# Splitting the last modulation of a mixer and expert block, and moving its gate half into the router steps

## The chip, the cores and the metric

The kernel runs on one core of a Trainium2 chip. The metric is the device time of one execution in microseconds (us); 1724.52 us is the median of three runs of the kernel before (1724.0 to 1725.7). The engines are TensorE (PE, with its weight loads as PEld), VectorE (DVE), ScalarE (ACT), GpSimd (POOL) and SyncE (SP), whose queue issues the large weight transfers. The core's 16 DMA engines share the transfers.

## The reference

A sequence of 256 tokens of width 1024 in fp32 passes two blocks. The first is conditioned on a vector `c`:

```
mod = (silu(c) @ w_ada + b_ada)            # 6 x 1024
shift1, scale1, gate1, shift2, scale2, gate2 = mod
h = rms_norm(x, norm1_g) * (1 + scale1) + shift1
proj = h @ w_in                            # conv, stick-breaking and forgetting attention
x = x + gate1 * (rms(y) * out_norm_g @ w_out)
h2 = rms_norm(x, norm2_g) * (1 + scale2) + shift2
logits = h2 @ router_w + router_b          # 32 experts, top 4, softmax of the four
out_e = swiglu(h2 @ w1_e + b1_e) @ w2_e + b2_e
x = x + gate2 * sum over experts of gate_e * out_e
```

The second block is a Fourier and convolution mixer, a gated feed-forward part, a pooling mixer, a second feed-forward part and a norm. `w_ada` is 1024 x 6144. An expert's weights are 1024 x 2048 and 1024 x 1024 values, 12.6 MB, and all 32 experts are read.

## The kernel before, in words

All large weights go through a ring of 14 places of 1 MB in on-chip memory. `ring_order` lists the units in the order in which SP issues them, and each unit takes the place of the one 14 before it. SP waits until that one has been used (`emptied`) and issues the new one; it does so strictly in order. The order of the first block is: `w_ada` third 0 (8 units), `w_in` (16), `w_ada` third 1 (8), `w_out` (4), `w_ada` third 2 (8), and then the experts. Of each expert there are eight units of the first matrix (`w1`) and four of the second (`w2`); the first two `w1` units of the next expert stand ahead of the `w2` units of this one. So `w1` units 0 and 1 of expert 0 take the places of `w_ada` units, and `w1` unit 2 of expert 1 takes the place of `w1` unit 0 of expert 0.

A third of `w_ada` is 2048 columns. An `ada_unit` multiplies 128 rows of it by 128 values of silu(c); its four matmuls of 512 columns go to four strips of 32 partitions of one bank (L478). Third 2 holds scale2 and gate2, third 1 holds gate1 and shift2. `mod_done` adds the bias (L1331).

Everything on an engine runs in program order, and semaphores tie the engines together. The stages that the change touches are:

- **Output projection.** Eight pieces (`out_piece`, L458 to L460, twelve matmuls each) accumulate in banks 0 to 3. ACT rounds a piece of `w_out` (L2114) and DVE takes the rest (L1315) into two buffers, so a piece can be prepared when the one two before it has been used. The eight `ada_unit` calls of third 2 stand between the pieces. Then the columns of shift2 and scale2 are turned into per-partition form (L734), piece 7 follows, gate2 is spread to 128 partitions (L740), and shift2 is multiplied with the router's weights (L746).
- **Residual.** DVE multiplies the four quarters by gate1 (L1686) and adds them to x (L1689). Ahead of that its program has the rest of the expert biases (L1665), two small constant matrices `J` and `S_` (L1667, L1669) and the slot numbers (L1670 to L1677).
- **Router.** PE transposes x (L757), multiplies by the router's weights (L764) and sums the parts (L769, "logits"). DVE finds the four best experts of each token (L1710 to L1729, "chosen"). PE counts each token's place in its expert (L772 to L774, "places"), and DVE makes the selection matrix of the first four experts (L1736, "ST"). PE gathers the tokens of experts 0 to 3 with 32 matmuls (L916, L921).
- **Expert 0.** PE starts with two `w1` units (L811), then counts the tokens of each expert (L932, L933), turns the places (L936), makes the slot row (L799) and the slot gates (L789) and turns the gates (L944). After that PE waits for DVE's copies of the turned gates (`gT`, L1847), reads the count of expert 0 into a register (`value_load`) and takes a branch: an expert with more than 64 tokens gets a second part. The branch ends with `skip` (L466), which adds to a semaphore from PE's instruction stream. A `w1` place is only free after the unit has been used and this second part has been run or skipped: for units 0 and 1 at the branch ahead of unit 2, for units 2 and 3 at the branch after unit 3, for units 4 to 7 at the branch after unit 7.

```
            if kind == "w1":
                return [name, ("w1b", name[1], (0, 0, 1, 1, 2, 2, 2, 2)[name[2]])]
```

## Time and profile before

| | us |
|---|---|
| median of 3 runs | 1724.52 |
| lowest, highest | 1724.0, 1725.7 |
| the profiled execution's own time | 1724.98 |
| its span | 1723.2 |
| PE busy | 1577.0 (92%) |
| DVE busy | 676.6 (39%) |
| ACT busy | 430.1 (25%) |

The span is the time from the first to the last instruction of the profiled execution; its own time is the one to which a time for the changed kernel can be compared, and it lies 0.46 us above the median. The page divides the span into 40 slices of 43 us. The experts run from about slice 5 to slice 27. The mean granted clock of TensorE is 0.973 of full speed. The queue of SP moves 530 of the 533 MB. A share of DMA of 1.0 (or slightly above, as it is modelled) means that all 16 engines move data all the time.

### The profile page before, as it was taken

Reading aid. Unit: us, or ns where it says so; the run is one execution under the profiler, and the core shown is the slowest. Engines: PE = TensorE matmul, PEld = TensorE weight load, DVE = VectorE, ACT = ScalarE, POOL = GpSimd, SP = SyncE. Lnnn points to the kernel's source line nnn. Section 1 sums busy time; section 2 is a strip of 40 time slices with the busy share of each in tenths; the row PEclk is TensorE's granted clock in tenths of the full one; section 3 lists DMA queues with packets and bytes.
Section 4 is the critical chain, followed back from the end, with each engine's and each line's share of the span. In section 5 each row is a group of like instructions: output and inputs, shape, how many; then the busy total and the mean of one; then the engine's idle time right before and its main releaser. Section 6 shows DMA issues by size and latency. Waiting matters only on the chain.

```text
span 1723.2 us, 21783 instructions
## 1 busy us (share of the span) xinstructions
PE 1577.0 (92%) x8617; PEld 884.4 (51%) x8617; DVE 676.6 (39%) x947; ACT 430.1 (25%) x670; POOL 43.1 (2%) x68
## 2 busy tenths in 40 slices
PE   6999899999999898999989888886998999889998
PEld 3887533333333223333223222224848998689986
DVE  3475522232312222232212212124766565356653
ACT  3564311101110000110101000003425444244443
POOL 3032000000000000000000000000000000000000
PEclk9999899999999999999999999997998999989999
DMA  9648979999999999999999999996335555355540
GB/s 362 184 162 303 372 283 418 415 417 416 415 417 415 417 416 416 417 415 417 415 415 415 410 418 412 415 407 215 121 122 171 181 186 192 101 167 179 192 147 25
DMA packets 151411, 533.46 MB, mean 310 GB/s; under 512 B 9693, under 2 KB 72820, under 8 KB 115280
## 3 DMA queue, kind: packets, MB, share of 16 engines
q1 hardware_dynamic: 149664, 530.18, 78.9%
q8 instruction: 123, 2.02, 0.5%
q0 software_dynamic: 1584, 0.94, 0.3%
q14 instruction: 40, 0.33, 0.1%
HBM read 530.02 MB, written 1.05 MB: 308 GB/s over the span
## 4 chain that ended last, share of the span: by engine, by line
PE 39%; DMA 14%; DVE 2%; ACT 1%; issue 1%; SPq 0%; DVEq 0%; ACTq 0%
DMA ring<-in_w_mlp 14%; PE ps L460 8%; PE ps L458 8%; PE ps L459 8%; PE ps L811 7%; PE ps L829 1%; PE ps L1199 1%; PE ps L836 1%; PE ps L1141 1%; PE ps L782 1%; PE ps L1280 1%; PE ps L1113 0%; PE ps L1294 0%; PE ps L1149 0%; DVE arena L2039 0%
## 5 line engine op out<-in xcount | busy, mean ns | idle before, releaser
L811 PE MATMUL ps<-ring,arena 128*64 128x512 f32 x2048 | 495.9, 606 | 25.6 <-DMA ring<-in_w_mlp 22.2
L811 PEld LDWEIGHTS ps<-ring,arena 128*64 128x64 f32 x2048 | 128.2, 136 | 273.0 <-issue 197.0
L829 PE MATMUL ps<-ring,arena 128*64 128x512 f32 x1024 | 239.0, 602 | 31.3 <-DMA ring<-in_w_mlp 26.6
L1315 DVE TENSOR_TENSOR wl<-ring,wh 128x1024 fp32r<-128x1024 f32 x132 | 161.3, 1225 | 138.4 <-ACT wh L2114 138.4
L458 PE MATMUL ps<-hth,wh 128*128 128x256 f32 x704 | 199.4, 283 | 1.3 <-DVE htl L1965 1.3
L460 PE MATMUL ps<-hth,wl 128*128 128x256 f32 x704 | 200.2, 284 | 0.0
L459 PE MATMUL ps<-htl,wh 128*128 128x256 f32 x704 | 198.6, 282 | 0.0
L1787 DVE TENSOR_TENSOR arena<-ps,arena 128x1024 f32<-128x1024 f32 x70 | 85.6, 1225 | 259.8 <-PE ps L836 246.1
L2114 ACT ACTIVATE wh<-ring 128x1024 fp32r<-128x1024 f32 x132 | 139.0, 1059 | 150.1 <-PE ps L460 150.1
L829 PEld LDWEIGHTS ps<-ring,arena 128*64 128x64 f32 x1024 | 69.4, 137 | 195.4 <-issue 122.4
L1807 DVE TENSOR_TENSOR arena<-ps,arena 128x512 f32<-128x512 f32 x34 | 23.5, 692 | 360.2 <-PE ps L829 357.0
L458 PEld LDWEIGHTS ps<-hth,wh 128*128 128x128 f32 x704 | 134.4, 191 | 2.0 <-DVE htl L1965 2.0
L459 PEld LDWEIGHTS ps<-htl,wh 128*128 128x128 f32 x704 | 134.9, 192 | 0.0
L460 PEld LDWEIGHTS ps<-hth,wl 128*128 128x128 f32 x704 | 134.1, 190 | 0.0
L2364 ACT ACTIVATE arena<-arena 128x512 f32<-128x512 f32 (+1 forms) x34 | 21.0, 617 | 318.1 <-DVE arena L1793 318.1
L2400 ACT ACTIVATE obh<-arena 128x512 fp32r<-128x512 f32 x30 | 18.9, 630 | 317.0 <-DVE arena L1807 317.0
L458 PE MATMUL ps<-wh,fth 128*128 128x512 f32 x176 | 69.8, 396 | 0.0
L459 PE MATMUL ps<-wl,fth 128*128 128x512 f32 x176 | 69.6, 396 | 0.0
L460 PE MATMUL ps<-wh,ftl 128*128 128x512 f32 x176 | 69.5, 395 | 0.0
L2348 ACT ACTIVATE arena<-ps,arena 128x256 f32<-128x256 f32 x60 | 30.5, 559 | 138.5 <-PE ps L782 131.5
L458 PE MATMUL ps<-wp,ht 128*128 128x384 f32 (+1 forms) x128 | 46.3, 362 | 3.8 <-DVE ht L1379 2.3
L460 PE MATMUL ps<-wp,ht 128*128 128x384 f32 (+1 forms) x128 | 44.6, 348 | 0.0
(409 smaller groups left out, 1761.2 us busy)
## 6 DMA issues: line engine op xcount, KB each, us to landing
ring<-in_w_mlp SPq DMA_DIRECT2D x384, 1024.0 KB, 21.4
ring<-in_w_ada SPq DMA_DIRECT2D x24, 1024.0 KB, 14.2
ring<-in_ffn_w_gate SPq DMA_DIRECT2D x22, 1024.0 KB, 5.2
ring<-in_ffn_w_up SPq DMA_DIRECT2D x22, 1024.0 KB, 5.2
ring<-in_ffn_w_down SPq DMA_DIRECT2D x22, 1024.0 KB, 4.8
ring<-in_w_in SPq DMA_DIRECT2D x10, 768.0 KB, 12.4
ring<-in_w_in_ab SPq DMA_DIRECT2D x6, 1024.0 KB, 12.3
ring<-in_w_out SPq DMA_DIRECT2D x4, 1024.0 KB, 8.0
```

Source lines behind the costliest of these rows:

```text
L458: pe.matmul(o, lh, rh, start=first, stop=False)
L459: pe.matmul(o, lh, rl, start=False, stop=False)
L460: return pe.matmul(o, ll, rh, start=False, stop=last)
L811: t = pe.matmul(PS[64 * g:64 * g + 64, HB[hb][ns], :], x[:, k8, :], u[:, f:f + 512], start=False, stop=k8 == 7)
L829: t = pe.matmul(PS[64 * g:64 * g + 64, 3, :], a4[:, kc, 64 * kg:64 * kg + 64], u[:, c, g * 512:(g + 1) * 512], start=k8 == 0, stop=k8 == 7)
L1315: dve.tensor_tensor(l, src, h.bitcast(F32), ALU.subtract).then_inc(*V.tick((st, "lo", n)))
L1787: dve.tensor_tensor(x, PS[:, b:b + 2, :], x, ALU.add).then_inc(*tick(name))
L1807: dve.tensor_tensor(OBF, PS[:, bank, :], G2R, ALU.mult).then_inc(*tick(n_f))
L2114: act.activation(h, src, ACT.Copy).then_inc(*S.tick((st, "hi", n)))
L2348: act.activation(XGT[b % 2][:, k, :], PS[:, bank, (k % 2) * 256:(k % 2) * 256 + 256], ACT.Identity, scale=a2[:, k:k + 1], bias=sh2[:, k:k ...
L2364: act.activation(SIG[:, 0:n], GLU[:, 0:n], ACT.Sigmoid, scale=1.702).then_inc(*Q.tick(name))
L2400: act.activation(OBH[0], OBF, ACT.Copy).then_inc(*S.same())
```

## The change

Third 2 of `w_ada` is read as two halves, `scale2` and `gate2`, of four units each. A unit is again 1 MB, but 256 rows by 1024 columns. The new function `ada_half` multiplies such a unit with four matmuls of 512 columns: strips 0 and 2 take the even 128 rows, strips 1 and 3 the odd ones, and `S_` (here a matrix that adds the two strips of a half) joins them when the result is turned or spread. The same number of bytes is read.

- The four `scale2` units stand ahead of pieces 3, 4, 5 and 6. The turn of scale2 and shift2 moves behind piece 7, in between the transposes of x.
- The four `gate2` units move into the router: two behind the logits, one behind the token counts, one behind the gather. Their sum goes to bank 3, and its bias is loaded again by GpSimd into part 0 of `modr`, once that has been used and zeroed (`ab2`).
- DVE makes `J` and `S_` at the very start and the slot numbers in the projection stage; the rest of the biases goes between two pieces of `w_out`.
- The token counts and the turn of the places move ahead of the gather. The rest of h (`h_rest`) for tokens 0 to 127 moves ahead of "pos".
- Spreading gate2 and turning the gates move behind the branch that frees the places of `w1` units 0 and 1, and PE's wait for `gT` moves into the loop over the experts; so do DVE's copies of the gates and the product with `b2`.
- GpSimd issues six bias transfers instead of four at the start, and two more with a memset of 128 x 512 values later.

```diff
-    order += ... [("out", kk) for kk in range(4)] + [("ada", 2, k) for k in range(8)]
+    order += ... [("out", kk) for kk in range(4)] + [(w, k) for w in ("scale2", "gate2") for k in range(4)]

+            def ada_half(name, k, bank):
+                u = rows_of((name, k), 2)
+                pe.wait_ge(*landed((name, k)))
+                for q in range(2):
+                    for c in range(2):
+                        p = 64 * q + 32 * c
+                        t = pe.matmul(PS[p:p + 32, bank, :], cTp[:, 2 * k + c, :], u[:, c, q * 512:(q + 1) * 512],
+                                      start=k == 0, stop=k == 3)
+                t.then_inc(*P.tick((name, k)))
...
+            pe.wait_ge(*done("cB"))
             for i in range(2):
                 t = pe.matmul(PS[:, 1, i * 32:(i + 1) * 32], parts[:, i * 128:(i + 1) * 128], J, start=True, stop=True)
             t.then_inc(*P.tick("logits"))
+            ada_half("gate2", 0, 3)
+            ada_half("gate2", 1, 3)
             pe.wait_ge(*done("chosen"))
...
+            pe.matmul(PS[0:1, 1, 0:32], CT(C_ONE, 1), gt[:, 0, :], start=True, stop=False)
+            pe.matmul(PS[0:1, 1, 0:32], CT(C_ONE, 1), gt[:, 1, :], start=False, stop=True).then_inc(*P.tick("counted"))
+            ada_half("gate2", 2, 3)
+            pe.wait_ge(*done("pos"))
...
+            ada_half("gate2", 3, 3)
             pe.wait_ge(*done("SB1 0"))
             pe.wait_ge(*done("B1S"))
+            pe.wait_ge(*done("cnt"))
             mlp1_bias(0, 0)
...
-            for i in range(2):
-                t = pe.transpose(PS[0:32, 2, 256 + i * 128:384 + i * 128], gate[:, i, :], ident)
-            t.then_inc(*P.tick("gate turned"))
-            pe.wait_ge(*done("gT"))
...
             second_gather(0, here > CAP)
             second_start(0, here > CAP)
+            pe.wait_ge(*done(("xgt", 0, 2)))
+            for g in range(2):
+                t = pe.matmul(PS[64 * g:64 * g + 64, 6, :], S_[:, g, 0:1].bitcast(F32).to_broadcast([128, 64]),
+                              modr[:, 0, :], start=True, stop=True)
+            t.then_inc(*P.tick("gate2"))
+            for i in range(2):
+                t = pe.transpose(PS[0:32, 2, 256 + i * 128:384 + i * 128], gate[:, i, :], ident)
+            t.then_inc(*P.tick("gate turned"))
...
+            pool.wait_ge(*done("mod turned"))
+            pool.memset(modr[:, 0, :], 0.0).then_inc(*G.tick("mod 0 zeroed"))
+            pool.wait_ge(*done("mod 0 zeroed"))
+            for q in range(2):
+                small("ab2", modr[64 * q:64 * q + 1, 0, :], I["b_ada"][:, 5120 + 512 * q:5632 + 512 * q])
...
-            for k in range(8):
-                ada(2, k)
+            for w, c in (("scale2", 4096), ("gate2", 5120)):
+                for k in range(4):
+                    fill_rows((w, k), I["w_ada"][0], k * 256, 2, c, 1024)
```

PE's program before, from the last matmul of output piece 6 to the first two of piece 7; L734 turns shift2 and scale2:

```order
L460 MATMUL ps<-wo_63,yl 128x512
L734 MATMUL ps<-arena 128x2 x8
L458 MATMUL ps<-wo_65,yh 128x512
L459 MATMUL ps<-wo_66,yh 128x512
L460 MATMUL ps<-wo_65,yl 128x512
```

And from the last matmul of piece 7 to the logits (L769), with the spreading of gate2 (L740), the shift's logits (L746, L747), the transposes of x (L757), the constant row (L760) and the router's product (L764):

```order
L460 MATMUL ps<-wo_65,yl 128x512
L740 MATMUL ps<-arena 64x512 x2
L746 MATMUL ps<-arena 32x1 x8
L747 MATMUL ps<-arena 32x1
L757 MATMUL ps<-arena 128x128 x16
L760 MATMUL ps<-arena 128x32
L764 MATMUL ps<-arena 32x256 x8
L769 MATMUL ps<-arena 128x32 x2
```

PE's program now, from the last matmul of piece 7 to the logits (now L784); L745 turns scale2, L752 is half of the transposes of x, L760 now turns shift2, L776 is the router's product:

```order
L460 MATMUL ps<-wo_65,yl 128x512
L745 MATMUL ps<-s,arena 128x2 x4
L752 MATMUL ps<-arena 128x128 x8
L760 MATMUL ps<-arena 128x2 x4
L752 MATMUL ps<-arena 128x128 x8
L770 MATMUL ps<-arena 32x1 x8
L771 MATMUL ps<-arena 32x1
L776 MATMUL ps<-arena 32x256 x8
L779 MATMUL ps<-arena 128x32
L784 MATMUL ps<-arena 128x32 x2
```

The turn of both rows stood ahead of piece 7; now it is in two parts behind it, and the spreading of gate2 is gone from this place.

PE's program before, from the logits to the branch of expert 0 (L957 reads the count); L772 to L774 are the places, L916 and L921 the gather, L811 the first two `w1` units, L932 and L933 the counts, L936 turns the places, L799 and L789 make slot row and slot gates, L944 turns the gates:

```order
L769 MATMUL ps<-arena 128x32 x2
L772 MATMUL ps<-arena 128x32
L773 MATMUL ps<-arena 128x32
L774 MATMUL ps<-arena 128x32
L916 MATMUL ps<-st,hh 128x256 x16
L921 MATMUL ps<-st,hl 128x256 x16
L804 MATMUL ps<-b1s,sb_83 128x512 x2
L811 MATMUL ps<-ring,arena 64x512 x8
L932 MATMUL ps<-arena 1x32
L933 MATMUL ps<-arena 1x32
L936 MATMUL ps<-arena 32x128 x2
L799 MATMUL ps<-post,s 128x256
```

The same stretch now, up to the gather; L718 is `ada_half`, L789 to L791 the places, L793 and L794 the counts, L798 turns the places:

```order
L784 MATMUL ps<-arena 128x32 x2
L718 MATMUL ps<-ring,arena 32x512 x8
L789 MATMUL ps<-arena 128x32
L790 MATMUL ps<-arena 128x32
L791 MATMUL ps<-arena 128x32
L793 MATMUL ps<-arena 1x32
L794 MATMUL ps<-arena 1x32
L718 MATMUL ps<-ring,arena 32x512 x4
L798 MATMUL ps<-arena 32x128 x2
L941 MATMUL ps<-st,hh 128x256 x16
```

And from the gather to the read of the count (L975); L829 is the bias, L836 the first two `w1` units, L824 and L814 slot row and slot gates:

```order
L946 MATMUL ps<-st,hl 128x256 x16
L718 MATMUL ps<-ring,arena 32x512 x4
L829 MATMUL ps<-b1s,sb_83 128x512 x2
L836 MATMUL ps<-ring,arena 64x512 x8
L824 MATMUL ps<-post,s 128x256
L814 MATMUL ps<-arena,st 64x1 x16
L975 TENSOR_LOAD arena
```

Three gate units and the counting steps now stand ahead of the gather, the fourth gate unit behind it, and nothing is left between the slot gates and the read of the count.

## Rows read from the trace of the kernel before

**Rows 1.** The page, part 2, what the DMA engines moved.

```profile
GB/s 362 184 162 303 372 283 418 415 417 416 415 417 415 417 416 416 417 415 417 415 415 415 410 418 412 415 407 215 121 122 171 181 186 192 101 167 179 192 147 25
```

**Rows 2.** Busy time by stretch: each engine's, granted clock, DMA share, GB/s.

```profile
196.00:210.00 14.00, 9.38 (x47) 6.65 (x46) 9.37 (x31) 8.14 (x16) 0.00 (x0) 0.50 1.01 409
210.00:212.00 2.00, 2.00 (x12) 2.00 (x12) 1.61 (x5) 0.00 (x0) 0.00 (x0) 0.56 0.40 158
212.00:224.00 12.00, 8.52 (x79) 4.89 (x79) 5.33 (x14) 1.97 (x4) 0.00 (x0) 0.92 0.01 1
224.00:226.00 2.00, 2.00 (x6) 0.67 (x7) 0.69 (x1) 0.00 (x0) 0.00 (x0) 0.50 0.52 119
...
234.00:240.00 6.00, 6.00 (x29) 1.78 (x29) 2.55 (x3) 1.28 (x1) 0.00 (x0) 1.00 0.61 220
240.00:260.00 20.00, 19.47 (x94) 6.94 (x92) 4.50 (x7) 3.07 (x6) 0.00 (x0) 1.00 1.01 397
```

**Rows 3.** PE in order of time, last expert: start, duration, idle before.

```profile
1160.93 1.94 PE L811 MATMUL ps<-ring,arena 128*64 128x512 f32 x8 [0.52 <-DMA ring<-in_w_mlp]
```

**Rows 4.** Waits of SP's queue, 195 to 260 us: total, times, longest.

```profile
SPq L2624 <- PEq L466: 44.3, 4, 29.5
```

**Rows 5.** PE in order of time, from the logits to expert 0.

```profile
202.64 1.03 PE L769 MATMUL ps<-arena 128*128 128x32 f32 x4 [0.71 <-DVE arena L1701]
206.00 0.64 PE L772 MATMUL ps<-arena 128*128 128x32 f32 x2 [2.33 <-DVE arena L1729]
...
208.53 3.59 PE L916 MATMUL ps<-st,hh 128*128 128x256 f32 x16 [1.04 <-DVE st L1736]
211.96 2.07 PE L921 MATMUL ps<-st,hl 128*128 128x256 f32 x16
...
214.42 3.65 PE L811 MATMUL ps<-ring,arena 128*64 128x512 f32 x16
...
219.42 1.12 PE L789 MATMUL ps<-arena,st 128*64 128x1 f32 x32
...
223.85 6.10 PE L811 MATMUL ps<-ring,arena 128*64 128x512 f32 x16 [2.98 <-PEq L466]
```

**Rows 6.** PE in order of time, the output projection.

```profile
156.55 1.06 PE L478 MATMUL ps<-ring,arena 128*32 128x512 f32 x8
...
182.11 1.92 PE L478 MATMUL ps<-ring,arena 128*32 128x512 f32 x16
...
186.86 1.84 PE L734 MATMUL ps<-arena 128*128 128x2 f32 x16
188.56 0.49 PE L458 MATMUL ps<-wo,yh 128*128 128x512 f32 x1
```

**Rows 7.** DVE in order of time, from the bias rest to the residual.

```profile
189.02 2.47 DVE L1665 TENSOR_TENSOR b1s<-arena,b1s 32x1024 fp32r<-32x1024 f32 x2
...
192.85 0.69 DVE L1686 TENSOR_TENSOR arena<-ps,arena 128x512 f32<-128x512 f32 x1
...
197.64 0.69 DVE L1689 TENSOR_TENSOR arena<-arena 128x512 f32<-128x512 f32 x1
```

**Rows 8.** PE in order of time, the first `w_ada` unit of the program.

```profile
7.00 1.93 PE L478 MATMUL ps<-ring,arena 128*32 128x512 f32 x8 [2.92 <-DMA ring<-in_w_ada]
```

**Rows 9.** DVE in order of time, the copies of the turned gates.

```profile
221.12 0.85 DVE L1847 COPY arena<-ps 32x256 f32<-32x256 f32 x2
```

**Rows 10.** DVE and POOL in order of time, where work moves to.

```profile
14.04 0.15 DVE L1344 TENSOR_SCALAR arena<-arena 128x1 f32<-128x1 f32 x1 [8.16 <-ACT arena L2128]
...
85.49 0.56 DVE L1387 COPY arena<-ps 128x384 f32<-128x384 f32 x1 [2.34 <-PE ps L460]
...
41.39 1.39 POOL L2561 MEMSET arena<- 128x1536 f32 x1 [26.35 <-DVE ht L1379]
```

**Rows 11.** POOL and PE, the gains issued last and first used.

```profile
10.59 0.96 POOL L2538 DMA_DIRECT2D arena<-in_fox_k_g  x2
...
26.23 0.26 PE L500 MATMUL ps<-arena 4*128 4x4 f32 x1
```

More of the change, by code:

```diff
@@ L114, in ring_order @@
     first = len(order)
-    order += [("ada", 1, k) for k in range(8)] + [("out", kk) for kk in range(4)] + [("ada", 2, k) for k in range(8)]
+    order += [("ada", 1, k) for k in range(8)] + [("out", kk) for kk in range(4)] + [(w, k) for w in ("scale2", "gate2") for k in range(4)]
     order += [("w1", 0, 0), ("w1", 0, 1)]
@@ new lines, in _, with x_turn @@
+            t.then_inc(*P.tick("scale2 turned"))
+            def x_turn(i, ns):
+                pe.wait_ge(*done(("x1", i, ns)))
+                for k in range(4 * ns, 4 * ns + 4):
+                    b, o = 4 + k // 2, (k % 2) * 256 + i * 128
+                    t = pe.transpose(PS[:, b, o:o + 128], X[:, i, k * 128:(k + 1) * 128], ident)
+                    if i == 1 and k % 2:
+                        t.then_inc(*P.tick(("x turned", k // 2)))
+            pe.wait_ge(*done(("yL", 3)))
+            x_turn(0, 0)
@@ L738, in _ @@
+            x_turn(1, 0)
+            for cc in range(4):
+                t = pe.matmul(PS[:, 6, 2 * cc:2 * cc + 2], modr[:, 1, cc * 128:(cc + 1) * 128], ident[:, 64:128:32],
+                              start=True, stop=True)
+            t.then_inc(*P.tick("shift2 turned"))
+            pe.wait_ge(*done("a2"))
             pe.wait_ge(*done("s2"))
-            for g in range(2):
-                t = pe.matmul(PS[64 * g:64 * g + 64, 5, :], sel_w(2 + g)[:, 0:64], modr[:, 2, :], start=True, stop=True)
@@ L748, in _ @@
+            pe.matmul(PS[0:32, 1, 100:101], rbrow, CT(C_ONE, 1, 0, 1), start=False, stop=True).then_inc(
                 *P.tick("shift logits"))
-            P = sig["pe_route"]
-            for ns in range(2):
-                pe.wait_ge(*done("Jc" if ns else "G2R"))
-                for i in range(2):
-                    pe.wait_ge(*done(("x1", i, ns)))
-                    for k in range(4 * ns, 4 * ns + 4):
-                        b, o = 4 + k // 2, (k % 2) * 256 + i * 128
-                        t = pe.transpose(PS[:, b, o:o + 128], X[:, i, k * 128:(k + 1) * 128], ident)
-                        if i == 1 and k % 2:
-                            t.then_inc(*P.tick(("x turned", k // 2)))
@@ L760, in _ @@
-            pe.matmul(PS[:, 1, 64:96], CT(C_ONE, 128, 0, 32), Jc, start=True, stop=True).then_inc(*P.tick("shifts"))
             for k in range(8):
@@ L2358, in _ @@
             xgt(0, 2, 6)
+            act.wait_ge(*done("gate2"))
+            act.activation(G2R, PS[:, 6, :], ACT.Copy).then_inc(*S.tick("G2R"))
             S, S2 = sig["act_moe"], sig["act_moe2"]
```

173 lines of the change are left out of this document (92 added, 81 removed).

## The prediction

> **What bounds the kernel now.** I read the page's row of what the DMA engines moved first [rows 1]. From slice 8 to slice 26 it stands at 407 to 420 GB/s, and in the stretch just behind the start of expert 0 the share is 1.01 [rows 2]. So the experts' weights set the pace, and every microsecond in which the stream stands still ahead of them is a microsecond of the kernel. At the end of that stage PE still waits 0.52 us for each unit to land, as ahead of the last but one `w1` unit [rows 3]; so the stage ends when the stream ends, and what follows it hangs on that.
>
> Then I looked for the place where the stream stands still. The busy time by stretch shows it [rows 2]: a share of 1.01 until 210, 0.40 in 210 to 212 (1.2 us idle), 0.01 in the next 12 us (11.9 us), 0.52 in 224 to 226 (1.0 us), and 0.61 in 234 to 240 (2.4 us). The first pause is 14.1 us, the second 2.4, together 16.5 us, and that is the most that any change at this place can give. The waits of SP's queue say what ended the first pause: one wait of 29.5 us for PE's own queue at L466, which is `skip` [rows 4]. The ring is full, and the next transfer (unit 2 of expert 1) needs the place of unit 0 of expert 0, which is free when PE gets to the branch of expert 0. PE's first matmul behind that branch is at 223.85 [rows 5], and the data start within 224 to 226 [rows 2]. So the question is how much earlier PE gets to this branch.
>
> **The change part by part.** Ahead of the router, six edits have one answer. Output piece 7 starts at 188.56 [rows 6]. Ahead of it go four of eight `w_ada` units, 0.96 us each (two in 1.92), and the turn, 1.70 us from 186.86 to 188.56 [rows 6]: 5.5 us. The first of these units covers a wait for the rounded input of piece 0, of which I give back 0.5 us as an estimate. The pieces come 5.0 us earlier, if ACT and DVE prepare `w_out` as fast; piece 7 starts at 183.6.
>
> DVE starts the residual at 192.85, although the first quarter is there one quarter of a piece after 188.56, at about 189.4. Until then it does the bias rest (2.47 us from 189.02, until 191.49) and constants and slot numbers (1.36 us, until 192.85) [rows 7]. The residual ends at 198.33 (197.64 and 0.69) [rows 7]. With DVE free at that place it starts near 184.6. It is no longer a chain of its own: it has to stop for scale2 and shift2, which PE turns behind piece 7 (2.95 us long, so from 186.6; 0.85 us each at the level of [rows 6], half of 1.70) and between the transposes. That puts its end at 191.0, or 191.8 if TensorE's clock has fallen: 6.6 to 7.3 us earlier. Two small steps become serial behind it (the router's shift product ahead of the parts, and the copy of the constant row ahead of the logits), 0.2 us each as an estimate from the 0.17 to 0.4 us of such steps. **Logits: 6.2 us earlier.** The ends are 5.0, if DVE waits again, and 6.8.
>
> Two gate units stand between the logits and the places. The logits start at 202.64 and the places at 206.00, with PE idle for 2.33 us of that, while DVE finds the experts [rows 5]: a gap of 3.36 us from start to start. The granted clock is 0.50 from 196 to 210 [rows 2], TensorE's lower level of 1.2 GHz. Half the clock makes 1.92 us of a unit's 0.96, and the program's first unit did take 1.93 us [rows 8], so I take 1.93. Then 1.03 and 3.86 are 4.9 us against 3.36: **1.5 us later.** At the upper level (2.4 GHz, 0.96 us each) the gap holds them and the cost is 0.
>
> From the places to the gather it is 2.53 us now (206.00 to 208.53) [rows 5]. The counts, the third gate unit and the turn of the places come in between. At the lower level: places 1.5, counts 0.3, unit 1.93, turn 0.8, which is 4.5 and so 2.0 later; at the upper level they fit behind DVE's steps, 0 later. I take the middle, **1.0 later**.
>
> The gather's first half runs 3.43 us (208.53 to 211.96) and the second 1.90 (211.96 to 213.86, where 2.07 is its own duration), because the clock rises in 211 to 212 (0.56 in 210 to 212) [rows 2, 5]. PE does more dense work ahead of it now, so the rise may come sooner: 0 to 1.5 us gained, **0.7 earlier**. The fourth gate unit costs **1.0 later** (0.96 to 1.93).
>
> Behind the two `w1` units, which end at 218.07, the slot gates start at 219.42 [rows 5]. In between stand counts, the turn, a wait for its copy and the slot row. Only the slot row stays, at most 0.4 us: **1.0 earlier**.
>
> The slot gates end at 220.54. The turn of the gates and the wait for DVE's copies (221.12 and 0.85, until 221.97) [rows 9] stand ahead of the read of the count. Both go behind the branch: 1.4 us, and the read may start while the slot gates run, so **1.6 earlier** (1.4 to 2.1).
>
> The sum at the branch is -6.2 + 1.5 + 1.0 - 0.7 + 1.0 - 1.0 - 1.6 = -6.0 us. With every clock term at its slow end it is -6.2 + 1.5 + 2.0 + 1.9 - 1.0 - 1.4 = -3.2 (-2.0 if the logits come only 5.0 us earlier); with every one at its fast end it is -6.8 - 1.5 + 1.0 - 1.0 - 2.1 = -10.4.
>
> The second pause depends on how long PE takes from the branch to unit 7 of expert 0. The gate2 product and the turn of the gates stand there now, some 1.5 us; against that, the clock is at 0.50 in 224 to 226 [rows 2] and two units took 6.10 us instead of 3.65 [rows 5]. If PE stays at the upper level, these 2.5 us are gone. I count 0, with -1.0 to +1.5.
>
> What else moves is hidden. `J` and `S_` go to DVE's start, where it is idle for 8.16 us ahead of 14.04; the slot numbers go into the 2.34 us that DVE waits ahead of 85.49; GpSimd's memset and two bias transfers go into 26.35 us of idle time ahead of 41.39 [rows 10]. Two more transfers stand ahead of the gains on GpSimd's queue, about 1.0 us by the 0.96 us of a pair; the last gains are issued by 11.55 and PE uses them at 26.23 [rows 11]. If all this cover failed, the start would come about 1 us later, at a stage that is not bound by the stream.
>
> The gate2 units hold four ring places longer, and in the queue they stand ahead of `w2` of expert 0. SP is in order, so the stream may now stop for them. The last one is used behind the gather, near 209.5; its place is filled within 5 us, by 214.5, and the branch comes at 217 or later. The stream then pauses in two parts with the same sum, and nothing is lost. Each microsecond that this last unit came later than 212 would cost one.
>
> **The clock rule.** The row shows the level rising after the dense gather began and staying low while PE did short steps with gaps [rows 2, 5]. The Trainium skill (TensorE: Matmul & The Clock Gate, Part 1: The HAM clock gate) says that the throttled level is the default and that activity releases it. By that rule, filling the gaps with gate units raises the clock sooner, and the sum would be the fast end. The trace agrees on the direction but does not show how much filling is enough.
>
> **Rivals.** (a) The fast case: the upper level from the gate units on. The gaps that held PE at 0.50 [rows 2] are filled with matmuls of 512 columns; against it, the places, counts and turns between them are tiny. Time: 1724.98 - 10.4 + 0.5 for part of the new work behind the branch = 1715.1, 1714.6 as a median. (b) The gate units sit on the router's path at the lower level, and new steps behind the branch lengthen the second pause: -3.2 + 1.0 = -2.2, 1722.8, or 1722.3 as a median. For it speaks that two units of 1.93 us do not fit into the idle 2.33 us [rows 5, 8]. (c) The change doesn't do what it says: DVE's or ACT's preparation of `w_out` becomes the pace of the pieces, and the gate units eat the rest. Time: 1724. A piece takes 2.95 us (188.56 to 191.5) and only the wait for DVE's last step is near it. (d) Slower: the clock does not rise in the gather and stays low through unit 7. The second half of the gather costs 1.5 more, bias and two units 4.1, and the way from the branch to unit 7 (15 us, of which 5 ran low) 10 more, which lengthens the second pause. -3.2 + 1.5 + 4.1 + 10 = +12, so 1737. It turns the sign as soon as the low level costs 3.2 us more than the slow end counts. Against it: the clock rose in 211 to 212, with dense work only since 208.53 [rows 2, 5].
>
> **Numbers.** The forecast is 1724.98 - 6.0 = 1719.0 against the profiled execution; the median lies 0.46 lower, so 1718.5. Chances: forecast (4.5 to 7.5 us faster) 0.52, (a) 0.20, (b) 0.17, (c) 0.06, (d) or another loss 0.05. The range reaches to (a) and most of (b): 1714.3 to 1721.8. This kernel's measurement tells about 0.2% from no change, 3.4 us. Faster than that are the forecast, (a) and half of (b): 0.82; within it half of (b) and most of (c): 0.13; slower 0.05.
>
> **What would show it.** Logits at 196 to 197; the places 4.5 to 5 us after them if the clock is low, 3.4 if not; the gather within 203 to 206; no wait for `gT` ahead of the branch; first matmul of unit 2 near 219, behind four of gate2; SP's longest wait for L466 shorter by 6; the first pause near 8 us, perhaps split in two; share 1.0 from 233 on, and the expert stage unchanged in length. It is wrong if the pieces of the projection wait for DVE, if the logits come later than 198, or if the second pause grows by more than 2 us.

## The result, and the profile after

The changed kernel takes 1711.02 us (median of five runs, 1708.66 to 1715.36) against 1724.0 us of the kernel before: a ratio of 0.9926, 95% interval 0.9907 to 0.9945. Two later series on other occasions gave 0.9937 (0.9924 to 0.9949) and 0.9928 (0.9914 to 0.9942). So it is 13.0 us faster in this series, and 11.4 and 12.1 us in the two later ones. The forecast was 6.0 us faster (1718.5), with a range that ended at 1714.3. The direction was right and so were most of the steps; the size was off by a factor of about two, and at one step, the branch of expert 0, a part of the mechanism was missed. The profiled execution shown here has 1711.02 us and a span of 1709.2 us.

The page's row of what the DMA engines moved, in 40 slices, answers to [rows 1]:

```profile
GB/s 363 184 166 296 386 394 416 416 417 414 417 415 416 417 415 417 416 415 417 415 416 413 411 416 412 415 401 210 99 124 178 190 182 188 108 163 186 184 148 25
```

The sixth slice (214 to 256 us) had 283 and has 394. From there to slice 26 the two rows agree within 3 GB/s. The busy time by stretch (PE, PEld, DVE, ACT, POOL, then granted clock, DMA share, GB/s) answers to [rows 2]:

```profile
196.00:210.00 14.00, 14.00 (x101) 7.24 (x94) 8.67 (x26) 2.82 (x8) 0.00 (x0) 0.94 1.01 410
210.00:212.00 2.00, 1.03 (x34) 0.98 (x34) 0.55 (x2) 0.00 (x0) 0.00 (x0) 1.00 0.24 90
212.00:224.00 12.00, 12.00 (x57) 4.09 (x59) 4.50 (x7) 2.10 (x5) 0.00 (x0) 1.00 0.87 348
224.00:226.00 2.00, 2.00 (x12) 0.43 (x8) 0.00 (x0) 0.99 (x1) 0.00 (x0) 1.00 0.69 156
234.00:240.00 6.00, 6.00 (x30) 2.01 (x28) 0.00 (x0) 0.00 (x0) 0.00 (x0) 1.00 1.01 412
```

The long pause from 210 to 225 has shrunk to one of 2.7 us (210.4 to 213.2), and a second of 1.1 us stands at 222 to 227. Added up microsecond by microsecond from 198 to 262, the share leaves 17.4 us unused before and 4.8 us after. That is 12.6 us, nearly the whole result. The granted clock is the other thing to read: 0.50 over the 14 us of the router before, 0.94 now, and 1.00 from 210 on, where it was 0.50 in 224 to 226. The waits of SP's queue (185 to 250 us; total, times, longest) answer to [rows 4]; the longest for the branch was 29.5 us and is 6.4, and the longest of all, 13.3, is now for a gate unit (L718). Such a wait need not be a pause of the stream, since the queue runs ahead of the data: from 198 to 209 the share is 1.0, and the first pause comes at 210.

```profile
SPq L2674 <- PEq L466: 27.9, 6, 6.4
SPq L2675 <- PE ps L718: 19.0, 3, 13.3
```

PE in order of time from the last turn of the attention (L486) to unit 2 of expert 0 (start, duration, idle before) answers to [rows 5 and 6]:

```profile
154.34 1.97 PE L486 MATMUL ps<-arena 128*128 128x128 f32 x16
...
185.62 0.95 PE L745 MATMUL ps<-s,arena 128*128 128x2 f32 x8
...
189.87 0.66 PE L752 MATMUL ps<-arena 128*128 128x128 f32 x4 [0.65 <-DVE arena L1722]
...
191.29 1.94 PE L776 MATMUL ps<-arena 128*32 128x256 f32 x16
...
194.16 1.03 PE L784 MATMUL ps<-arena 128*128 128x32 f32 x4 [0.38 <-DVE arena L1737]
195.13 3.19 PE L718 MATMUL ps<-ring,arena 128*32 128x512 f32 x16
198.25 0.41 PE L789 MATMUL ps<-arena 128*128 128x32 f32 x2
...
200.25 2.17 PE L941 MATMUL ps<-st,hh 128*128 128x256 f32 x16
202.26 2.08 PE L946 MATMUL ps<-st,hl 128*128 128x256 f32 x16
204.27 1.07 PE L718 MATMUL ps<-ring,arena 128*32 128x512 f32 x8
...
209.82 1.12 PE L814 MATMUL ps<-arena,st 128*64 128x1 f32 x32
211.91 1.08 PE L980 MATMUL ps<-arena,s 128*64 128x512 f32 x4 [0.97 <-PEq L466]
...
213.24 3.65 PE L836 MATMUL ps<-ring,arena 128*64 128x512 f32 x16
```

The gather's first half took 3.59 us and takes 2.17; the pair of `w1` units behind the branch took 6.10 and takes 3.65. DVE's residual, its first and its last step, answers to [rows 7]. In the kernel before it started at 192.85 and ended at 198.33; now it ends at 189.81:

```profile
183.84 0.69 DVE L1719 TENSOR_TENSOR arena<-ps,arena 128x512 f32<-128x512 f32 x1 [1.72 <-PE ps L460]
...
189.12 0.69 DVE L1722 TENSOR_TENSOR arena<-arena 128x512 f32<-128x512 f32 x1
```

**A measure that is sharper than the median.** The runs of one kernel are spread over 3 to 9 us. The profiles show where much of the spread between them arises: ahead of the stages that are compared here. I call that part the front. PE's program is the same there in all kernels (DVE and GpSimd have the small hidden moves in some), and its last step is the turn at L486. It starts at 154.34 in the profile above and at this time in the kernel before:

```profile
154.65 1.97 PE L486 MATMUL ps<-arena 128*128 128x128 f32 x16
```

Over the 16 profiled executions of this study it starts between 151.96 and 156.01. The time of the profiled execution less this start is 1570.33 us before, and 1556.68, 1556.85, 1556.75 and 1556.72 us in four executions of the changed kernel. I call it the rest. It repeats within 0.2 us in these four, and within 0.6 us in two executions of another kernel below, so steps of one to two microseconds can be told, with the reservation that all other kernels, the one before among them, were profiled once. The pauses of the stream support it: the rest less the unused time of the table's last column lies between 1550.3 and 1553.9 us in all 16. By the rest the change is worth 13.6 us. Of the differences between the two profiles, 0.3 us come from the front. The medians of the three series give less, 11.4 to 13.0 us. Whether the moves on DVE and GpSimd make the front of the changed kernel about 1 us longer stays open: its starts spread over 4 us, and only three profiles are of kernels with the front as before.

### The profile page after: what moved, and what is told of

Read it like the earlier page. It is cut to its first block, busy times and chain, and to the rows that moved or that the text cites. A ratio compares the mean times of both kernels' runs of the same rounds, so it can differ in the third digit from the quotient of the medians.

```text
span 1709.2 us, 21793 instructions
## 1 busy us (share of the span) xinstructions
PE 1568.9 (92%) x8617; PEld 881.3 (52%) x8617; DVE 677.2 (40%) x948; ACT 430.6 (25%) x670; POOL 45.6 (3%) x73
## 3 DMA queue, kind: packets, MB, share of 16 engines
HBM read 530.02 MB, written 1.05 MB: 311 GB/s over the span
## 4 chain that ended last, share of the span: by engine, by line
PE 39%; DMA 14%; DVE 2%; ACT 1%; issue 1%; SPq 0%; DVEq 0%; ACTq 0%
DMA ring<-in_w_mlp 14%; PE ps L460 8%; PE ps L458 8%; PE ps L459 8%; PE ps L836 7%; PE ps L854 1%; PE ps L1228 1%; PE ps L861 1%; PE ps L1170 1%; PE ps L807 1%; PE ps L1309 1%; PE ps L1142 0%; PE ps L1323 0%; PE ps L1178 0%; DVE arena L2082 0%
## 5 line engine op out<-in xcount | busy, mean ns | idle before, releaser
L836 PE MATMUL ps<-ring,arena 128*64 128x512 f32 x2048 | 493.5, 603 | 22.4 <-DMA ring<-in_w_mlp 22.1
L836 PEld LDWEIGHTS ps<-ring,arena 128*64 128x64 f32 x2048 | 128.1, 136 | 267.8 <-issue 192.3
```

The costliest lines, as they stand in the source:

```text
L836: t = pe.matmul(PS[64 * g:64 * g + 64, HB[hb][ns], :], x[:, k8, :], u[:, f:f + 512], start=False, stop=k8 == 7)
```

## The experiments

| kernel | median us | ratio to before (95%) | start of L486 | rest | unused DMA 198:262 |
|---|---|---|---|---|---|
| before | 1724.0 | 1 | 154.65 | 1570.33 | 17.4 |
| changed | 1711.02 | 0.9926 (0.9907, 0.9945) | 154.34 | 1556.68 | 4.8 |
| changed again | 1712.8 | 0.9937 (0.9924, 0.9949) | 155.01 | 1556.85 | 5.2 |
| changed, third | 1711.18 | 0.9928 (0.9914, 0.9942) | 154.51 | 1556.75 | 4.4 |
| changed, fourth | 1710.98 (1 run) | - | 154.26 | 1556.72 | 4.8 |
| gate units late | 1715.07 | 0.995 (0.9937, 0.9963) | 155.24 | 1560.30 | 9.5 |
| gate units cut | 1712.48 | 0.9933 (0.992, 0.9946) | 154.16 | 1557.06 | 5.4 |
| before with filler | 1723.48 | 0.9997 (0.9988, 1.0006) | 153.74 | 1569.74 | 16.3 |
| DVE moves only | 1719.55 | 0.998 (0.9964, 0.9995) | 155.05 | 1566.92 | 13.0 |
| late steps only | 1718.27 | 0.9969 (0.9958, 0.998) | 152.44 | 1564.36 | 12.2 |
| branch step back | 1712.82 | 0.9943 (0.9931, 0.9955) | 151.96 | 1560.34 | 8.2 |
| all units early | 1715.42 | 0.9952 (0.9939, 0.9965) | 155.26 | 1560.34 | 8.4 |
| one unit between turns | 1711.77 | 0.9927 (0.9914, 0.9941) | 154.83 | 1556.89 | 4.8 |
| the same, second | 1710.08 (1 run) | - | 153.81 | 1556.27 | 5.0 |
| last unit behind branch | 1711.53 | 0.993 (0.9916, 0.9943) | 156.01 | 1557.15 | 6.4 |
| both moves | 1714.1 | 0.9948 (0.9934, 0.9961) | 153.09 | 1557.03 | 6.7 |

**What does the clock do?** My theory after the result was that the gate units brought the upper level back early (clock theory). The rival was that only the order of PE's work counts, each unit at its own length. First the changed kernel once more, as the measure.

> The changed kernel once more, beside the kernel before and the three next kernels on one chip. Both theories expect 1711 +- 3 us, 12 to 14 us less than before. In the profile the first time gave TensorE's lower level only from about 191 to 197 us; if the time of the fall and rise moves with the run, the gather should start within 199 to 203 us, and the kernel's time should vary with it by 2 to 4 us.

The profile came as expected (gather at 200.98), and the gain of 11.4 us lies a little under the 12 to 14 foreseen. Then all four gate units behind the gather:

```diff
-            ada_half("gate2", 0, 3)
-            ada_half("gate2", 1, 3)
...
+            for k in range(4):
+                ada_half("gate2", k, 3)
```

> The changed kernel with all four gate2 units behind the gather instead of two behind the logits, one behind the counts and one behind the gather. Clock theory (the units keep TensorE busy and bring its clock up ahead of the gather): the places come 0.7 us earlier, but the granted clock stays at 0.50 into the gather, which takes 5.3 us instead of 4.0; with 2.9 us of units more behind it the branch is 4 to 5 us later, 1715 to 1716 us. Order theory (only where the work stands counts, the clock is the same): the gather takes 4.0 us, the branch is 2 to 3 us later, 1713 to 1714 us.

```profile
198.40 0.64 PE L787 MATMUL ps<-arena 128*128 128x32 f32 x2 [2.34 <-DVE arena L1763]
...
200.93 3.78 PE L938 MATMUL ps<-st,hh 128*128 128x256 f32 x16
204.51 2.58 PE L943 MATMUL ps<-st,hl 128*128 128x256 f32 x16
207.02 3.64 PE L718 MATMUL ps<-ring,arena 128*32 128x512 f32 x32
```

Behind the last turn of the attention the places come after 43.16 us instead of 43.91, 0.75 us earlier, as expected; not more, since PE waits 2.34 us for DVE. The gather takes 6.1 us instead of 4.0, with the granted clock at 0.50 until 205. So behind the logits two of the units stand mostly in idle time, and what they cost beyond it the gather gives back. The first matmul behind the branch comes 4.5 us later, as the clock theory has it, and the rest is 3.6 us longer.

But the time is not lost by that path. Two rows of the stretch, with the columns as above (from 210 to 226 the share is 1.02, so no pause is left at the branch, whose first matmul is at 217.28):

```profile
203.00:204.00 1.00, 1.00 (x7) 1.00 (x6) 0.45 (x3) 0.00 (x0) 0.00 (x0) 0.50 0.00 0
212.00:213.00 1.00, 1.00 (x6) 0.29 (x4) 0.00 (x0) 0.00 (x0) 0.00 (x0) 1.00 1.00 410
```

The stream runs dry from 200 on, stands still from 203 to 209 and goes on while the gate units are used (from 207.02); SP's longest wait here is 23.4 us for L718. The gate units hold their ring places longer, and SP is strictly in order. Of the 3.6 us, the slow gather explains at most 2.1, by an estimate from 6.1 less 4.0; the rest of the loss is where the units stand.

Next the kernel before with 12 dead matmuls of 512 columns, eight behind the logits and four behind the places:

```diff
+            filler(2)
             pe.wait_ge(*done("chosen"))
...
+            filler(1)
```

> The kernel before with twelve matmuls more whose result nobody reads: two units' worth (four matmuls of 512 columns each) behind the logits, one behind the places, where the changed kernel has its gate2 units. Nothing else is changed. Clock theory: the granted clock is up at the gather, which takes about 4.0 us instead of 5.3; the fillers cost 1 to 2.5 us at the lower level, so 1723 to 1725 us in spite of the added work, and 2 us less if the clock also stays up behind the branch. Order theory: the fillers cost what they take, 2.5 to 3 us, and the gather is as before: 1727 us.

PE around them, and then the busy time by stretch, with the columns as above:

```profile
202.72 3.64 PE L775 MATMUL ps<-arena 128*32 128x512 f32 x16
206.29 0.64 PE L779 MATMUL ps<-arena 128*128 128x32 f32 x2
...
207.32 1.06 PE L775 MATMUL ps<-arena 128*32 128x512 f32 x8
208.43 2.18 PE L924 MATMUL ps<-st,hh 128*128 128x256 f32 x16
```

```profile
197.00:206.00 9.00, 7.86 (x43) 3.36 (x42) 5.11 (x24) 6.37 (x12) 0.00 (x0) 0.50 1.01 411
207.00:211.00 4.00, 3.86 (x30) 2.71 (x30) 3.51 (x6) 0.00 (x0) 0.00 (x0) 1.00 0.68 273
```

4.7 us of added PE work cost nothing (ratio 0.9997; rest -0.6). The kernel before had 0.50 in 207 to 211; here it has 1.00, and the gather takes 4.3 us instead of 5.3. That is as the clock theory has it (4.0 us and 1723 to 1725 were expected), and the order theory (1727 us) is refuted. What I did not expect is that the filler alone gains so little: the clock fell again at the branch, from 220 to 227. The last of this group cuts the gate units to 32 columns, which leaves most of gate2's product out:

```diff
-                        t = pe.matmul(PS[p:p + 32, bank, :], cTp[:, 2 * k + c, :], u[:, c, q * 512:(q + 1) * 512],
+                        n = 32 if name == "gate2" else 512
+                        t = pe.matmul(PS[p:p + 32, bank, 0:n], cTp[:, 2 * k + c, :], u[:, c, q * 512:q * 512 + n],
```

> The changed kernel with the gate2 units' matmuls cut from 512 to 32 columns, which leaves most of gate2 out; order, waits and transfers are the same. Clock theory: TensorE has 3 us less of dense work, the clock stays at 0.50 into the gather (5 us instead of 4.0), and the branch comes at about the same time, 0 to 1 us earlier: 1710 to 1711.5 us. Order theory: the branch comes 2.5 us earlier, as much as the units took on the path: 1708.5 us.

The level stays at 0.50 from 191 to 204, the gather takes 6.0 us (199.91 to 205.88), and the kernel with about 4 us less of matmuls is not faster: rest +0.3, median 1712.48 where 1710 to 1711.5 was expected. Its branch comes 1.0 us later (58.56 us behind the last turn instead of 57.57). Gate units of full length cost this kernel nothing on balance.

**Which part of the change brings what?** Three experiments do or undo one group of edits each; a fourth undoes the split.

```diff
# before, with these moved on DVE: J and S_ to the start, slot numbers
# into the hidden layers, the bias rest ahead of output halves 6 and 7
```

> The kernel before, with DVE's five moves alone: J and S_ at the start, slot numbers in the hidden layers, the bias rest ahead of output halves 6 and 7. PE's work is unchanged, piece 7 stays near 188.5. If the residual's late start was a term of its own (first theory), it starts at 189.5 to 190 instead of 192.85, the logits come 3 us earlier (199.5) and the median is near 1721.5. If the router was held by PE's own steps (gate2's product, the shift product and the turns of x) as much as by DVE (rival), the logits come at most 1 us earlier and the median is 1723 to 1724.

```profile
188.98 0.49 PE L458 MATMUL ps<-wo,yh 128*128 128x512 f32 x1
...
200.16 0.60 PE L769 MATMUL ps<-arena 128*128 128x32 f32 x4 [0.68 <-DVE arena L1704]
```

From the start of piece 7 to the logits it is 11.18 us, and it was 14.08: 2.9 us, as the first theory said, and the rest is 3.4 us shorter (median 1719.55, expected 1721.5). The changed kernel has 11.27. So DVE's late start was a term of its own, and by itself it is as large as all that the changed kernel gains between piece 7 and the logits.

```diff
# before, with counts and the turn of the places ahead of the gather,
# the rest of h split around the places, the turn of the gates, gT and
# B2 behind the branch; modulation as before
```

> The kernel before, with the late steps of the change alone: counts and the turn of the places ahead of the gather, DVE's rest of h split around the places, the turn of the gates with gT and B2 behind the branch. Nothing of the modulation moves, no gate unit stands in the router. If these steps are serial with the branch (first theory), the logits stay at 202.6, the branch comes 2.5 to 4.5 us earlier (first matmul 219.5 to 221.5) and the median is 1720 to 1721.5. If the clock decides (rival), the steps put ahead of the gather lengthen places to gather at the lower level by as much as they save later, and the median is 1723 to 1724.

```profile
216.25 1.12 PE L795 MATMUL ps<-arena,st 128*64 128x1 f32 x32
218.33 0.38 PE L957 MATMUL ps<-arena 128*32 128x128 f32 x2 [0.97 <-PEq L466]
218.64 3.65 PE L817 MATMUL ps<-ring,arena 128*64 128x512 f32 x16
```

```profile
210.00:226.00 16.00, 15.03 (x106) 7.24 (x104) 5.30 (x11) 3.19 (x7) 0.00 (x0) 1.00 0.40 158
226.00:240.00 14.00, 13.49 (x59) 4.20 (x59) 5.66 (x7) 2.51 (x3) 0.00 (x0) 1.00 0.98 402
```

This was the largest surprise: the rest is 6.0 us shorter, where 3 to 4.5 us were expected. From the last turn of the attention to unit 2 it is 66.20 us instead of 69.20, which is the 3.0 us of serial steps; 2.0 of them are idle time of PE, 0.97 us at the branch instead of 2.98. The other half stands behind the branch: the clock does not fall, the pair of units takes 3.65 us instead of 6.10, and the second pause is all but gone (share 0.98 in 226 to 240). The rival is refuted: places to gather is 2.54 us as before (203.84 to 206.38), counts and turn fit behind DVE's steps.

```diff
# changed, with gate2's product, the turn of the gates, gT and B2
# back ahead of the branch of expert 0
```

> The changed kernel, with gate2's product, the turn of the gates and the wait for DVE's copies put back ahead of the branch of expert 0. If the reordering at the branch is worth what the difference of the two kernels shows (1.0 to 2.4 us ahead of the branch, plus gate2's product, 0.9), the branch comes 2.5 to 3.5 us later than in the changed kernel (near 215) and the median is 1714 to 1716. If the wait for the copies was hidden behind the read of the count (rival), it comes at most 1 us later and the median is 1711 to 1713.

```profile
207.50 1.12 PE L814 MATMUL ps<-arena,st 128*64 128x1 f32 x32
208.45 1.08 PE L966 MATMUL ps<-arena,s 128*64 128x512 f32 x4
...
212.74 5.27 PE L836 MATMUL ps<-ring,arena 128*64 128x512 f32 x16 [2.89 <-PEq L466]
```

The idle time is 2.89 us again, the clock falls again (0.58 in 212 to 216), and the pair takes 5.27 us. From the slot gates to unit 2 it is 5.24 us instead of 3.42, and the rest is 3.6 us longer, as the first theory said. The median (1712.82) lies in the rival's range. In the profile this kernel's front ended 2.4 us early; whether it did so in the other five runs isn't known. What speaks for the rest are the rows above and the unused time of the stream, 8.2 us against 4.8.

```diff
# changed, with the four gate2 units between output pieces,
# none in the router
```

> The changed kernel, with all eight units of scale2 and gate2 ahead of output piece 7, as many as before, and none in the router or the gather. Clock theory: piece 7 comes 3.8 us later than in the changed kernel (186.7), the router has gaps and stays at 0.50 until the gather has run, so that the gate units save nothing by leaving it: branch 3.5 to 5 us later than in the changed kernel, median 1715.5 to 1717. Order theory (the gate units cost the router their own length wherever they stand): the four units cost the same there as here, the branch moves less than 1 us and the median is 1711.5 to 1713.

```profile
198.92 1.04 PE L789 MATMUL ps<-arena 128*128 128x32 f32 x4 [0.38 <-DVE arena L1740]
202.29 0.63 PE L792 MATMUL ps<-arena 128*128 128x32 f32 x2 [2.33 <-DVE arena L1768]
...
204.82 3.79 PE L943 MATMUL ps<-st,hh 128*128 128x256 f32 x16
208.40 2.38 PE L948 MATMUL ps<-st,hl 128*128 128x256 f32 x16
```

The rest is 3.6 us longer, with a gather of 5.8 us (204.82 to 210.62). The first matmul behind the branch comes 4.3 us later (61.89 us behind the last turn), within the clock theory's 3.5 to 5, and here the stream does stand still until the branch (share 0.07 in 212 to 216). This is what the split brings, as a net value; the median, 1715.42, is just under the 1715.5 to 1717 expected.

The three parts add up: 3.4 (DVE) and 6.0 (late steps) done alone, 3.6 (split) undone alone, are 13.0 us of the 13.6. Since two were done alone and one was undone, the sum is a check of size and doesn't show that the parts are independent: the branch step alone, undone, costs 3.6 us again.

**Can it be made better, and is the fall of the clock an order of the code?** The changed kernel still runs 6 us at 0.50, from 191 to 197. I moved one gate unit between the turns of x, where PE waits 0.65 us for DVE, beside a third series of the changed kernel. In this kernel and in the last two below the banks of the gate product and of the places are swapped for it, which the excerpts of the code don't show.

```diff
             x_turn(0, 1)
+            ada_half("gate2", 0, 2)
             x_turn(1, 1)
...
-            ada_half("gate2", 0, 3)
-            ada_half("gate2", 1, 3)
+            ada_half("gate2", 1, 2)
```

> The changed kernel unchanged, as the measure for the run beside it. Both theories expect 1711 to 1713 us, logits 11.2 to 11.4 us behind the start of output piece 7, branch 29 us behind it, and the granted clock at 0.50 for 6 to 7 us around the logits.

> The changed kernel, with the first gate unit put between the last transposes of x, where PE waits for DVE and the clock is about to fall, one unit left between logits and places (banks of the gate product and of the places are swapped for it). Clock theory: the level does not fall, or only for 2 to 3 us; logits product and the unit run at the upper level, the places wait for DVE again, 3.0 to 3.4 us behind the logits instead of 4.1, and branch and unit 2 come 1 to 2 us earlier behind piece 7 than in the changed kernel; 0.5 to 2 us faster, 1710 to 1711.5. Rival (the unit only lengthens the way to the logits): the logits come 0.7 to 1 us later and the gap to the places is 0.7 shorter, the clock falls as before, within 0.5 us of the changed kernel.

Busy time by stretch in the first execution of this kernel, and then in the second:

```profile
187.00:203.00 16.00, 13.92 (x132) 9.80 (x133) 12.91 (x45) 9.18 (x19) 0.00 (x0) 1.00 1.01 418
212.00:215.00 3.00, 3.00 (x9) 0.82 (x10) 2.75 (x5) 0.60 (x1) 0.00 (x0) 0.50 0.86 337
```

```profile
187.00:196.00 9.00, 7.08 (x72) 3.93 (x71) 6.69 (x28) 7.39 (x14) 0.00 (x0) 1.00 1.01 418
197.00:200.00 3.00, 3.00 (x18) 1.21 (x19) 2.83 (x8) 0.00 (x0) 0.00 (x0) 0.50 1.00 412
```

In the first execution the level stays at 1.00 through the whole router, and slot gates and branch come 1.5 us earlier behind piece 7. Then it falls at 212, and the pair of units takes 5.10 us instead of 3.65: rest 1556.89, nothing won. The first pause is 1.2 us there and the second 2.7, in the changed kernel 2.7 and 1.1. The third series of the changed kernel had 1556.75. So I asked whether this fall belongs to the order of the work, with one more execution of each of the two kernels.

> The same kernel as one unit between the turns of x. If the fall of the level at the branch belongs to this order of work, it is there again at 212 to 216, and the pauses add up to 4.5 to 5 us; if it was chance (rival), the level stays and the pauses are 3 to 3.5 us, with a time of 1709 to 1711.

> The changed kernel unchanged, for the same comparison: clock at 0.50 around the logits and at 1.00 from 198 on through the branch, pauses of 4.4 to 5.2 us together, 1711 to 1713. If the level behind the branch is chance in this kernel too (rival), it falls there in this execution and the pauses are longer.

The same code was at 0.50 in 197 to 200 this time and not at the branch, rest 1556.27. In four executions of the changed kernel the fall always began at about 191 and never came at the branch. So the fall at the branch came in one of two executions of one kernel and in none of four of the other. Its place is not fixed by the program alone; how often the changed kernel can have it, four executions can't tell. The last two kernels put the last gate unit behind the branch, without and with the unit between the turns:

```diff
-            ada_half("gate2", 3, 3)
             pe.wait_ge(*done("SB1 0"))
...
             second_start(0, here > CAP)
+            ada_half("gate2", 3, 2)
```

> The changed kernel, with the last gate unit put behind the branch of expert 0 and gate2's product and the turn of the gates behind unit 2 of expert 0 (banks of gate product and places swapped). Theory (what counts is when PE passes the branch, and in the second pause how much PE has done by unit 7): the branch comes 1 us earlier behind output piece 7 than in the changed kernel (28.0 instead of 29.0 us), the first pause is 1 us shorter, the total of PE's work to unit 7 is the same and the second pause grows by as much: 1711 to 1713. If only the first pause counts (rival), 1709.5 to 1711.

> The kernel with one unit between the turns of x, and with the last gate unit behind the branch as well. The level fell there in that kernel, at 212, behind slot gates of one column and 0.97 us of idle, and the second pause took back what the router had won. If dense work right behind the branch keeps the level up, w1 unit 2 takes 3.65 us for its pair, the pauses add up to 3.3 us or less (4.4 to 5.2 in the changed kernel) and the median is 1709 to 1711. If the level falls all the same (rival), the pauses stay at 4.5 to 5 us and the median is 1711 to 1712.5.

```profile
212.53 1.14 PE L718 MATMUL ps<-ring,arena 128*32 128x512 f32 x8 [1.01 <-PEq L466]
```

```profile
210.00:213.00 3.00, 3.00 (x14) 0.77 (x8) 1.29 (x2) 0.00 (x0) 0.00 (x0) 0.57 0.38 104
```

The row of 212.53 is of the kernel with the last unit behind the branch: 56.52 us behind the last turn instead of 57.57, 1.05 earlier, and worth nothing (rest +0.4); its clock fell at 213, too. The first pause did not get 1 us shorter, as I expected, but longer: 5.1 us between 209 and 216. The second is 0.4 us. In 213 to 216 SP's wait of 11.3 us is for the last gate unit (L718), where in the changed kernel the wait that ended the pause was for the branch (L466, 6.1 us). That unit ended at 213.6, and until then nothing moved:

```profile
213.00:214.00 1.00, 1.00 (x10) 0.30 (x4) 0.48 (x1) 0.00 (x0) 0.00 (x0) 0.69 0.00 0
```

So this kernel is no test of what an earlier branch is worth: the place of the last gate unit stands ahead in the queue, and with the unit behind the branch the stream waits for it (in the kernel with both moves as well, 12.2 us). The row of 210 to 213 is of the kernel with both moves: the level fell although dense work stood right behind the branch, which refutes my theory there. By the rest it is level with the changed kernel (+0.3); the median, 1714.1, is above both ranges that I gave. No order that I tried beats the changed kernel.

## Why the prediction was wrong

The step that failed is the one at the branch. The prediction priced the removed wait for the turned gates by its length alone and put the pause behind it at 0; the runs show 6.0 us for the late steps where it has 2.6. Two more terms were mis-sized: the clock at the gate units, places and gather (2.9 us) and the way from piece 7 to the logits (1.6 us). Together with 0.4 us at the pieces these make the 7.6 us between 6.0 and 13.6.

The way to the branch, step by step; measured is the difference of the two profiles, cleaned of the 0.3 us of the front.

| step | forecast | measured |
|---|---|---|
| pieces of the output projection | -5.0 | -5.4 |
| piece 7 to the logits | -1.2 | -2.8 |
| two gate units ahead of the places | +1.5 | +0.7 |
| places to gather | +1.0 | -0.5 |
| gather | -0.7 | -1.3 |
| fourth gate unit | +1.0 | +1.0 |
| bias and two `w1` units | 0 | +0.1 |
| counts, turn, slot row | -1.0 | -1.1 |
| slot gates to the first matmul behind the branch | -1.6 | -2.3 |
| sum at the branch | -6.0 | -11.6 |
| behind it | 0 | -2.0 |

The last row is what is left of the 13.6 us; 1.3 of it is the second pause (2.4 to 1.1 us), and where the other 0.7 arise was not traced.

**Right, with the right size:** what bounds the kernel, the limit of the gain (16.5 us), the pieces, the fourth unit, and the counts. The hidden moves look hidden in this pair of profiles: behind the slot numbers DVE still waits 1.44 us of its 2.34 [rows 10], and the last turn of the attention starts at 154.34 against 154.65, though by the spread of that start 1 us can't be excluded. Of the pieces only the first waits for DVE, 0.63 us, near the 0.5 that I gave back, so rival (c) is out.

**Piece 7 to the logits, mis-sized by 1.6 us.** I let the residual end 6.6 to 7.3 us earlier; it ended 8.2 us earlier. I also added 0.4 us for two serial steps; from the residual's end to the logits it was 4.31 us and is 4.35. By its own numbers the prediction could have said 6.1 to 6.9 us for the logits (198.33 less 191.8 is 6.5, not 6.6) and took the low end. The run with DVE's moves alone shows 2.9 us for this term.

**The clock terms, 2.9 us.** Units ahead of the places, places to gather, and gather have the forecast +1.8 and measured -1.1. I took the lower level for the first and the middle for the next two. In fact the level rose between 197 and 198 (granted clock 0.63 there), within the second gate unit (3.19 us for two, not 3.86), and everything behind ran at the upper level. That is nearly the case of rival (a), which had a chance of 0.20 and has the upper level from the first unit on. The Trainium skill (TensorE: Matmul & The Clock Gate, Part 1: The HAM clock gate) has that activity releases the throttle; the trace agrees with the direction. I had set the fast end of the sum aside since no row of before showed how much filling is enough. By the run with filler, the kernel before has 1.00 in 207 to 211 with such matmuls and 0.50 without.

**The branch and what is behind it, 2.7 us.** This is the step whose mechanism I missed in part. I priced the removed wait at 1.4 to 2.1 us, and wrote that the 2.5 us of the pair at 0.50 would be gone if PE stayed at the upper level, but counted 0. The late steps alone brought 6.0 us where the forecast has 2.6 for them. In all four kernels with 2.9 to 3.1 us of idle time ahead of the first matmul behind the branch the clock fell there, within that time (before: idle from 220.86, 0.50 from 222 on); in twelve executions with 0.96 to 1.01 us it fell three times. So the removed wait cost not only its own length: with it the clock was down for the pair of units behind the branch. This link is seen in 16 profiles, and putting the step back brought both the idle time and the fall back; no run changed the idle time alone, and what decides in the three was not found.

**The rivals.** (a) was right in its mechanism, and 3.6 us short (1714.6 against 1711.0), since it too counted DVE's term and the second pause too low. (b) failed at its first clause: only the first gate unit and a part of the second ran at the lower level. (d) did not occur. The chances for a faster kernel add up to 0.81, not 0.82, which changes nothing. Of what I named as signs, the logits at 194.2 are ahead of the 196 to 197 foreseen, the places 4.1 us behind them, between the two marks; the gather starts at 200.25 and not at 203; unit 2 starts at 213.24, not near 219; no wait for `gT` is left, as written; and the first pause is 2.7 us instead of 8. The warning about the ring held: the last gate unit was used by 205.3 and the branch ended the pause, while in the kernels that used gate units later the stream waited for them. The 5 us to fill a place have no row behind them.

## What to carry to other kernels

Where a stage of short steps stands between the last transfer and the branch that frees the buffers, price each removed wait twice: by its length, and by what TensorE's clock does behind it; here a gap of 3 us ahead of dense work cost 1.7 to 3.0 us more than the time by which it delayed that work (rest against start of unit 2, step put back and late steps alone). Useful dense work put into such gaps can be free, and moving it out can cost. But such work may hold a buffer that the stream needs: with the units behind the gather or behind the branch the stream waited for them. Subtract the start of the last unchanged step from the profiled time before comparing variants: it turned a spread of several microseconds into 0.2 us here, in another kernel 0.6.

## What was not expected of the hardware

- The level fell at 191 in the changed kernel although PE was busy for 2.04 us of the 3 us ahead of 190, with no gap above 0.65 us between its instructions. What ran there were products with 2 columns and transposes. With one unit of 512-column matmuls between them it fell at 196 to 197 in two executions, and in one not before the branch. The stretch in the changed kernel, and then a longer one of the kernel with cut units, which stayed at 0.50 for 12 us while PE was busy for 9.57:

```profile
187.00:190.00 3.00, 2.04 (x18) 1.75 (x17) 2.51 (x5) 2.63 (x7) 0.00 (x0) 1.00 1.03 423
```

```profile
192.00:204.00 12.00, 9.57 (x73) 7.84 (x67) 7.66 (x30) 4.50 (x8) 0.00 (x0) 0.50 1.01 414
```

- 4.7 us of added matmuls in the kernel before cost no time that can be measured (ratio 0.9997, 0.9988 to 1.0006).
- The same program, run again, fell at another place: at 212 in one execution, at 197 in the next. Its rest changed by only 0.6 us: the late fall was paid behind the branch (5.10 us for the pair of units instead of 3.65), the early one in the router (branch 1.45 us later behind the last turn).
